# The inversion of a chunked delta-rule scan in 32x32 pieces, and channel sums taken with 32 weight columns

## The chip, the cores and the metric

The kernel runs on one core of one Trainium2 chip. The metric is the device time of one execution in microseconds; lower is better. The engines are TensorE (PE, with its weight loads listed apart as PEld), VectorE (DVE), ScalarE (ACT), GpSimd (POOL) and the DMA queues.

## The reference

One encoder layer over 1024 + 256 tokens of 1024 channels, in fp32. Its parts: an RMS norm; one input projection; 2-D neighbourhood attention; an RWKV-7 scan in both directions; projections and gates that merge the two branches; a squared-ReLU MLP. Only the scan is touched. Cut to it:

```
def step(S, inp):                       # for each head, N = 64, two directions
    r_t, w_t, k_t, v_t, a_t, b_t = inp
    sa = einsum('zdhij,zdhj->zdhi', S, a_t)
    S = S * w_t[..., None, :] + sa[..., :, None] * b_t[..., None, :] + v_t[..., :, None] * k_t[..., None, :]
    y = einsum('zdhij,zdhj->zdhi', S, r_t)
    return S, y

kk = kk * rsqrt(sum(kk * kk, axis=-1) + 1e-12)          # norm of k over the 64 channels of a head
y  = (y - mean) * rsqrt(var + GN_EPS) * ln_w + ln_b     # mean and variance over the same 64 channels
```

## The kernel before

The scan is `scan_mixer`. A pair of heads fills the 128 partitions (64 channels each), so 8 heads are 4 pairs (`CT`); the 1280 tokens are taken in 5 blocks of 256 (`NB`), and a block in 4 chunks of 64 tokens (`GR`, index `g`). Two directions run side by side (index `u`). That makes 20 steps (`q`), each with 4 chunks, each with 2 heads x 2 directions = four independent 64x64 problems.

Inside a chunk the recurrence becomes a triangular 64x64 system. It is inverted by doubling: Y starts as the exact inverse of the 2x2 blocks on the diagonal (mask `first`, L955), X is its transpose (`turn`, L556). Each of the 5 levels then doubles the size of the inverted diagonal blocks, from 2 to 4, 8, 16, 32 and at last 64. A level is

- `level_q` (L568): q = A^T X, four 64x64 products per chunk;
- a mask on DVE (L1053), which keeps the part of q that joins two blocks, giving Q1;
- `level_xy`: new X (L577) and new Y (L580) from Q1, four products each; the last level needs Y alone;
- a copy from PSUM to SBUF on ACT (L890; the last level L894), which the next level's q reads.

The order on PE is written out by hand. The four chunks are staggered, so that PE works on others while DVE and ACT have one: within level l it is q(0), xy of the level before for chunk 2, q(1), xy of the level before for chunk 3, q(2), xy(0), q(3), xy(1). Behind the levels come, for each chunk, the state products (L592 to L639), and between them the next block's Gram products (L525, `gram_products`) and transposes to tokens (L538 to L544). Their inputs are prepared by POOL (L429 to L462, `prepare`), which starts when the chunk's masks of the step before are done. DVE, ACT and POOL each execute their list in order.

Every matmul here is fp32; the profile lists it as two LDWEIGHTS and two MATMUL records. "64*64" in a row is the part of the array that is used, rows times columns of it.

Work on whole pairs is placed between levels of certain blocks (`side`, `side_late`). Two such jobs are norms over the 64 channels of a head, once for k (tile sc_nrm) and once for y (sc_std), for each of the 4 pairs. `by_head` (L650) multiplies each of ten 128-token tiles, as weights, with two columns of ones; ACT takes the square root of the 128x20 result; DVE inverts it (`inverse`, L960); POOL spreads it to 128x1280 (L466); `back` (L656) turns it with ten products with the identity. Six of the eight norms lie in block i = 1 of the loop; the first (k of pair 0) is ahead of the loop and the last (y of pair 3) behind it. In the loop `inverse` stands on DVE in level 2 between the masks of chunks 2 and 3.

Of the kernel before, what the change touches and what calls it, by code (L numbers as in the profile page):

```python
# [9 lines left out]
P = 128  # L10
# [24 lines left out]
GRAM_BANK, TOK_BANK, STATE_BANK, LORA_BANK = 4, 5, 6, 7  # L35
LEVELS = 5
DECAY = -0.6065306597126334
# [14 lines left out]
CN_N = 384  # L52
# [4 lines left out]
CS_I = CS_L + LEVELS * 2 * C  # L57
# [249 lines left out]
def scan_mixer(nc, lora, params, cn_scan, ident, ones, mean, sT):  # L307

    with ExitStack() as ctx:
# [3 lines left out]
        def sem(n):  # L313
# [7 lines left out]
        joins = cs[:, CS_L:CS_L + LEVELS * 2 * C].rearrange("p (l t) -> p l t", l=LEVELS)  # L321
        eye, neg_eye = cs[:, CS_I:CS_I + C], cs[:, CS_I + C:CS_I + 2 * C]
        wl = sb("sc_lora", [P, CT, 5, P])
        k1a, half_bias = sb("sc_k1a", [P, CT]), sb("sc_hb", [P, CT, 4])
        rk_ones = sb("sc_rk", [P, CT, P])
        norms = [sb(f"sc_n{n}", [P, 2 * NT]) for n in range(2)]
# [12 lines left out]
        XY = [sb(f"sc_xy{g}", [P, 2, 2, C]) for g in range(GR)]  # L339
        AI, Q1, PT, UT = ([sb(f"sc_{n}{g}", [P, 2, C]) for g in range(GR)]  # L340
# [6 lines left out]
        x_out = [units(g, 2 * C, C) for g in range(GR)]  # L347
        y_out = [units(g, 4 * C, C) for g in range(GR)]
# [4 lines left out]
        cs_in, lora_in, scaled = sem("cs_in"), [sem(f"lora_in{c}") for c in range(CT)], sem("scaled")  # L353
# [10 lines left out]
        sqk_ready, ss_ps, nrm_ready, rn_ready, rnb_ready, rnb_ps, kk_ready = (  # L364
            sem("sqk"), sem("ss_ps"), sem("nrm"), sem("rn"), sem("rnb"), sem("rnb_ps"), sem("kk"))
        mean_ps, yc_ready, sqy_ready, var_ps, std_ready, rs_ready, rsb_ready, rsb_ps, yn_ready = (
            sem("mean_ps"), sem("yc"), sem("sqy"), sem("var_ps"), sem("std"), sem("rs"), sem("rsb"),
# [5 lines left out]
        heads = (slice(0, HD), slice(HD, P))  # L373
        col = lambda ct, n: params[:, PM_RK + ct * NPC + n:PM_RK + ct * NPC + n + 1]
# [31 lines left out]

        def tiles_of(p):

            return range(GROUPS[p][0] // P, (GROUPS[p][0] + GROUPS[p][1]) // P)
# [9 lines left out]
        def _(pool):  # L419
# [44 lines left out]
            def spread(ready, turn, norm, buf, done):  # L464
                pool.wait_ge(ready, turn + 1)
                nc.gpsimd.tensor_copy(buf[:, :].rearrange("p (n t) -> p n t", t=C),  # L466
                                      norm[:, :].unsqueeze(2).to_broadcast([P, 2 * NT, C])).then_inc(done, 1)

# [12 lines left out]
            spread(rn_ready, 0, norms[0], nrm, rnb_ready)  # L481
            prepare(0)
            for q in range(STEPS):
                ct, i = divmod(q, NB)
                if q + 1 < STEPS:
                    prepare(q + 1)
                if i == 0 and ct > 0:
                    bonus_in(ct - 1)
                if i == 1 and ct > 0:
                    spread(rs_ready, ct - 1, norms[1], std, rsb_ready)  # L490
                if i == 1 and ct + 1 < CT:
                    spread(rn_ready, ct + 1, norms[0], nrm, rnb_ready)
                if i == 3 and ct > 0:
                    plus_bonus(ct - 1)
            bonus_in(CT - 1)
            spread(rs_ready, CT - 1, norms[1], std, rsb_ready)
# [3 lines left out]
        def _(pe):  # L500
# [48 lines left out]
            def turn(q, g):  # L549
# [4 lines left out]
                for u in range(2):  # L554
                    for rows in heads:
                        last = nc.tensor.matmul(x_out[g][rows, u, :], XY[g][rows, 1, u, :], eye[rows, :],  # L556
                                                start=True, stop=True)
                last.then_inc(x1_ps, 1)

            def level_q(q, l, g):  # L560
# [5 lines left out]
                for u in range(2):  # L566
                    for rows in heads:
                        last = nc.tensor.matmul(q_out[g][rows, u, :], AI[g][rows, u, :], XY[g][rows, 0, u, :],  # L568
                                                start=True, stop=True)
                last.then_inc(q_ps, 1)  # L570

            def level_xy(q, l, g):
                pe.wait_ge(q_ready, (q * LEVELS + l) * GR + g + 1)
                for u in range(2):
                    if l < LEVELS - 1:
                        for rows in heads:
                            nc.tensor.matmul(x_out[g][rows, u, :], XY[g][rows, 1, u, :], Q1[g][rows, u, :],  # L577
                                             start=True, stop=True)
                    for rows in heads:
                        last = nc.tensor.matmul(y_out[g][rows, u, :], Q1[g][rows, u, :], XY[g][rows, 1, u, :],  # L580
                                                start=True, stop=True)
# [66 lines left out]
            def by_head(bank, sq, sums, done):  # L648
                for n in range(NT):
                    last = nc.tensor.matmul(ps[:, bank, 2 * n:2 * n + 2], sq[:, n * P:(n + 1) * P],  # L650
                                            sums[:, 0:P:HD], start=True, stop=True)
                last.then_inc(done, 1)

            def back(bank, spread, p, done):
                for m, n in enumerate(tiles_of(p)):
                    last = nc.tensor.matmul(ps[:, bank, m * P:(m + 1) * P], spread[:, n * P:(n + 1) * P], ident,  # L656
                                            start=True, stop=True)
                last.then_inc(done, 1)

            def side(ct, i, l):  # L660
# [10 lines left out]
                if i == 1 and ct > 0 and l == 0:  # L671
                    pe.wait_ge(sqy_ready, ct * NG)
                    by_head(GRAM_BANK, std, mean, var_ps)
                if i == 1 and ct + 1 < CT and l == 1:
                    pe.wait_ge(tok_ready, n)
                    pe.wait_ge(sqk_ready, (ct + 2) * NG)
                    by_head(TOK_BANK, nrm, ones, ss_ps)
# [7 lines left out]
                if i == 2 and ct > 0 and p is not None:  # L685
                    if p == 0:
                        pe.wait_ge(rsb_ready, ct)
                    else:
                        pe.wait_ge(yn_ready, c * NG + 1)
                    back(GRAM_BANK, std, p, rsb_ps)  # L690
                if i == 3 and ct + 1 < CT and p is not None:
                    if p == 0:
                        pe.wait_ge(rnb_ready, ct + 2)
                    else:
                        pe.wait_ge(kk_ready, (ct + 1) * NG + 1)
                    back(GRAM_BANK, nrm, p, rnb_ps)
# [5 lines left out]
            def side_late(ct, i):  # L702
# [9 lines left out]
                if i == 2 and ct > 0:  # L712
                    back(TOK_BANK, std, 1, rsb_ps)
                if i == 3 and ct + 1 < CT:
                    back(TOK_BANK, nrm, 1, rnb_ps)
# [17 lines left out]
            by_head(GRAM_BANK, nrm, ones, ss_ps)  # L733
            lora_products(0, 0, 3)
            lora_products(0, 1, 3)
            pe.wait_ge(rnb_ready, 1)
            for p in range(NG):
                back(p, nrm, p, rnb_ps)
            pe.wait_ge(cs_in, 16)
# [6 lines left out]
            pe.wait_ge(kk_ready, NG)  # L746
# [60 lines left out]
            by_head(STATE_BANK, std, mean, var_ps)  # L807
            pe.wait_ge(rsb_ready, CT)
            for p in range(NG):
                back(p, std, p, rsb_ps)  # L810
# [5 lines left out]
        def _(act):  # L816
# [29 lines left out]
            def k_norm(ct, bank):  # L846
                act.wait_ge(ss_ps, ct + 1)
                nc.scalar.activation(norms[0][:, :], ps[:, bank, 0:2 * NT], ACT.Sqrt,
                                     bias=params[:, PM_EPS + 2:PM_EPS + 3]).then_inc(nrm_ready, 1)

            def y_std(ct, bank):
                act.wait_ge(var_ps, ct + 1)
                nc.scalar.activation(norms[1][:, :], ps[:, bank, 0:2 * NT], ACT.Sqrt,
                                     bias=params[:, PM_EPS + 1:PM_EPS + 2]).then_inc(std_ready, 1)
# [25 lines left out]
            for q in range(STEPS):  # L880
                ct, i = divmod(q, NB)
                more, ahead = q + 1 < STEPS, q + 2 < STEPS
                for g in range(GR):
                    act.wait_ge(x1_ps, q * GR + g + 1)
                    nc.scalar.activation(XY[g][:, 0, :, :], x_out[g], ACT.Copy).then_inc(x1_ready, 1)
                for l in range(LEVELS):
                    for g in range(GR):
                        act.wait_ge(xy_ps, (q * LEVELS + l) * GR + g + 1)
                        if l < LEVELS - 1:
                            nc.scalar.activation(  # L890
                                XY[g][:, :, :, :].rearrange("p n u t -> p (n u t)"),
                                ps[:, g, 2 * C:6 * C], ACT.Copy).then_inc(xy_ready, 1)
                        else:
                            nc.scalar.activation(XY[g][:, 1, :, :], y_out[g], ACT.Copy  # L894
# [1154 lines left out]
```

## Time and profile before

| | us |
|---|---|
| median of 3 runs (lowest, highest) | 2915.7 (2912.87, 2916.56) |
| the profiled execution, its own time | 2910.93 |
| its span, first to last instruction | 2909.2 |
| of the span: the scan's loop of 20 steps, 950 to about 1645 | about 695 |

| engine | busy us | share of the span |
|---|---|---|
| PE | 2653.8 | 91% |
| PEld | 2209.6 | 76% |
| DVE | 1241.4 | 43% |
| ACT | 668.9 | 23% |
| POOL | 827.3 | 28% |

The table says that PE works almost all the time. It does not say what a row of PE is made of: how much of a matmul's time is its columns and how much is the wait for results of DVE and ACT has to be read from the stretch of the scan itself. Times in the rows are microseconds from the start of the span, "ns" apart.

### The profile page before, as it was taken

To read this page: it belongs to the slowest core of one execution; us is meant where nothing else is said; L and a number is where in the kernel's file an instruction comes from. 1 tells how busy PE (TensorE), PEld (TensorE's weight loads), DVE (VectorE), ACT (ScalarE), POOL (GpSimd) and SP (SyncE) were. 2 spreads that over 40 slices of the span, in tenths; PEclk is the share of its full clock that TensorE was granted. 3 is DMA by queue.
4 is the path that set the end of the run, shared out by engine and by line. 5 is a ranking of instruction groups with operands and counts; after the bars stand their busy time and mean duration, and the time that the engine had idled before them with its cause. 6 is when DMAs were issued, how large, how long until landed. Compare 5 with 4: busy or idle time off the path is not lost. (4 is left out here: it accounts for less than half of the span.)

```text
span 2909.2 us, 68114 instructions
## 1 busy us (share of the span) xinstructions
PE 2653.8 (91%) x29216; PEld 2209.6 (76%) x29216; DVE 1241.4 (43%) x2236; ACT 668.9 (23%) x1544; POOL 827.3 (28%) x644
## 2 busy tenths in 40 slices
PE   3987997997997999999999799596999999999997
PEld 2885456886886899998989655485888888888886
DVE  5003663551111444444444322565445544544545
ACT  3101551110001444444444211131011001101102
POOL 1222113332332233232333000543233233333324
PEclk9998998998998999999999999798999999999999
DMA  4111102101221000000000143432011111101113
GB/s 119 42 44 38 32 17 81 42 22 62 86 85 57 4 4 4 3 4 3 4 3 4 40 152 116 150 123 80 29 43 36 36 36 43 36 29 50 36 43 130
DMA packets 60191, 143.10 MB, mean 49 GB/s; under 512 B 12112, under 2 KB 31184, under 8 KB 59472
## 3 DMA queue, kind: packets, MB, share of 16 engines
q1 hardware_dynamic: 46176, 114.36, 12.0%
q10 hardware_dynamic: 10256, 12.49, 1.4%
q0 software_dynamic: 3552, 13.11, 1.1%
q8 instruction: 177, 2.90, 0.4%
q14 instruction: 30, 0.25, 0.0%
HBM read 108.48 MB, written 31.46 MB: 48 GB/s over the span
## 5 line engine op out<-in xcount | busy, mean ns | idle before, releaser
L1905 DVE TENSOR_TENSOR f<-f,ff_pd 128x512 f32<-128x512 f32 x320 | 214.2, 684 | 153.2 <-PE ff_pd L94 153.1
L1891 DVE TENSOR_TENSOR ff_sq<-ff_rl 128x512 f32<-128x512 f32 (+1 forms) x96 | 102.8, 1071 | 295.6 <-ACT ff_rl L1852 295.6
L1852 ACT ACTIVATE ff_rl<-ff_pu 128x512 f32<-128x512 f32 (+1 forms) x96 | 50.6, 527 | 759.0 <-PE ff_pu L94 759.0
L580 PE MATMUL sc_ps<-sc_xy,sc_q 64*64 64x64 f32 x3200 | 198.1, 221 | 0.0
L1053 DVE TENSOR_TENSOR sc_q<-sc_ps,sc_cs 128x128 f32<-128x128 f32 x400 | 113.6, 290 | 163.5 <-PE sc_ps L568 162.5
L577 PE MATMUL sc_ps<-sc_q,sc_xy 64*64 64x64 f32 x2560 | 170.6, 222 | 0.0
L568 PE MATMUL sc_ps<-sc_xy,sc_ai 64*64 64x64 f32 x3200 | 160.0, 223 | 1.4 <-ACT sc_xy L890 0.9
L890 ACT ACTIVATE sc_xy<-sc_ps 128x256 f32<-128x256 f32 x320 | 122.5, 383 | 160.3 <-PE sc_ps L580 159.7
L580 PEld LDWEIGHTS sc_ps<-sc_xy,sc_q 64*64 64x64 f32 x3200 | 156.1, 137 | 2.1 <-issue 1.0
L94 PE MATMUL ff_pu<-h2h,ff_wu0h 128*128 128x512 f32 (+1 forms) x384 | 136.8, 356 | 14.2 <-POOL ff_wu0l L1800 14.2
L429 POOL TENSOR_SCALAR sc_fac<-sc_icl,params,sc_k1a 128x512 f32<-128x512 f32 x20 | 15.3, 767 | 432.3 <-DVE sc_xy L955 414.5
L568 PEld LDWEIGHTS sc_ps<-sc_xy,sc_ai 64*64 64x64 f32 x3200 | 125.6, 137 | 15.3 <-ACT sc_xy L890 11.8
L94 PE MATMUL ff_pu<-h2l,ff_wu0h 128*128 128x512 f32 (+1 forms) x384 | 136.5, 356 | 0.0
L94 PE MATMUL ff_pu<-h2h,ff_wu0l 128*128 128x512 f32 (+1 forms) x384 | 136.5, 356 | 0.0
L94 PE MATMUL ff_pu<-h2l,ff_wu1h 128*128 128x512 f32 (+1 forms) x384 | 136.0, 354 | 0.0
L94 PE MATMUL ff_pu<-h2h,ff_wu1h 128*128 128x512 f32 (+1 forms) x384 | 135.9, 354 | 0.0
L94 PE MATMUL ff_pd<-ff_wd0h,ff_gh 128*128 128x512 f32 x320 | 126.6, 395 | 10.2 <-DVE f L1905 10.2
L94 PE MATMUL ff_pu<-h2h,ff_wu1l 128*128 128x512 f32 (+1 forms) x384 | 135.8, 354 | 0.0
L577 PEld LDWEIGHTS sc_ps<-sc_q,sc_xy 64*64 64x64 f32 x2560 | 132.3, 138 | 1.3
L1797 POOL TENSOR_TENSOR ff_wd0h<-ff_wr,params 128x1024 fp32r<-128x1024 f32 x16 | 30.3, 1895 | 356.4 <-PE ff_pd L94 356.4
L94 PE MATMUL ff_pd<-ff_wd1h,ff_gh 128*128 128x512 f32 x320 | 124.7, 390 | 0.0
L94 PE MATMUL ff_pd<-ff_wd0l,ff_gh 128*128 128x512 f32 x320 | 124.7, 390 | 0.0
(275 smaller groups left out, 7246.3 us busy)
## 6 DMA issues: line engine op xcount, KB each, us to landing
ff_wr<-in_w_up SPq DMA_DIRECT2D x32, 512.0 KB, 3.2
ff_wr<-in_w_down SPq DMA_DIRECT2D x32, 512.0 KB, 3.2
g_dram<-gp_g ACTq DMA_DIRECT2D x16, 640.0 KB, 2.9
mb_gate<-g_dram SPq DMA_DIRECT2D x8, 1280.0 KB, 8.9
gp_w<-in_w_in SPq DMA_DIRECT2D x16, 512.0 KB, 3.5
sp_w<-in_w_in SPq DMA_DIRECT2D x15, 512.0 KB, 3.5
n_x<-in_x SPq DMA_DIRECT2D x10, 512.0 KB, 3.6
m_dram<-mb_mo POOLq DMA_DIRECT2D x8, 640.0 KB, 8.9
```

The lines of the kernel that those rows point to most:

```text
L94: mm = nc.tensor.matmul(out, stationary[a], moving[b], start=first and n == 0, stop=last and n == len(pairs) - 1)
L429: nc.gpsimd.tensor_scalar(fac[:, :, :], icl[:, :, :], col(ct, K_A), k1a[:, ct:ct + 1], ALU.mult, ALU.add).then_inc(prep_own, 1)
L568: last = nc.tensor.matmul(q_out[g][rows, u, :], AI[g][rows, u, :], XY[g][rows, 0, u, :], start=True, stop=True)
L577: nc.tensor.matmul(x_out[g][rows, u, :], XY[g][rows, 1, u, :], Q1[g][rows, u, :], start=True, stop=True)
L580: last = nc.tensor.matmul(y_out[g][rows, u, :], Q1[g][rows, u, :], XY[g][rows, 1, u, :], start=True, stop=True)
L890: nc.scalar.activation(XY[g][:, :, :, :].rearrange("p n u t -> p (n u t)"), ps[:, g, 2 * C:6 * C], ACT.Copy).then_inc(xy_ready, 1)
L1053: nc.vector.tensor_tensor(Q1[g][:, :, :].rearrange("p u t -> p (u t)"), ps[:, g, 0:2 * C], joins[:, l, :], ALU.mult).then_inc(q_ready, 1)
L1797: nc.gpsimd.tensor_tensor(to[0], wr[m % 2][:, :], zero_like(wr[m % 2][:, :], zero), ALU.add).then_inc(high_done, 1)
L1852: nc.scalar.activation(rl[u % 2][:, 0:tn], pu[b][:, 0:tn], ACT.Relu).then_inc(relu, 1)
L1891: nc.vector.tensor_tensor(sq[u % 2][:, 0:tn], rl[u % 2][:, 0:tn], rl[u % 2][:, 0:tn], ALU.mult).then_inc(squared, 1)
L1905: nc.vector.tensor_tensor(at, at, pd[d % 4][:, :], ALU.add).then_inc(added, 1)
```

## The change

Up to the fourth level all that is computed lies in the 32x32 blocks on the diagonal. The change computes only those, in tiles of 32x32 of the array.

- A 64x64 product becomes two of 32x32. The four "strips" of 32 partitions (two per head) use the four tiles on the diagonal of the array. `turn`, `level_q` and `level_xy` of levels 0 to 3 have eight products where they had four. Results are packed: X and Y of a chunk are 128x64 each (`XYQ`), so the ACT copy reads 128x128 where it read 128x256, and the DVE mask works on 128x64 where it worked on 128x128.
- Level 3 writes its 32x32 results into places in a 64x64 area of PSUM whose other parts are zero. The area is zeroed once ahead of the loop (a DVE memset of 128x1024, and PE waits on it). Its copy is 128x256 as before. Level 4 is as before, in 64x64.
- `by_head` is three products: the tokens are the moving operand (512 columns each), the weights are 32 columns of which two are used, and the results go to partitions 0, 32 and 64. ACT's square root and DVE's reciprocal then work on 96x512 where they worked on 128x20.
- POOL's spread is gone. `back` multiplies two rows of each piece with two rows of ones and gives 128 partitions x 512 (or 256) columns at once, one product where there were four (or two).

```
+        strips = [(slice(s * Q, (s + 1) * Q), slice(s % 2 * Q, (s % 2 + 1) * Q)) for s in range(4)]
...
                 for u in range(2):
-                    for rows in heads:
-                        last = nc.tensor.matmul(q_out[g][rows, u, :], AI[g][rows, u, :], XY[g][rows, 0, u, :],
-                                                start=True, stop=True)
+                    if l < LAST_LEVEL:
+                        for rows, own in strips:
+                            last = nc.tensor.matmul(qq_out[g][rows, u, :], AI[g][rows, u, own],
+                                                    XYQ[g][rows, 0, u, :], start=True, stop=True)
...
+                    for n, (small, wide) in enumerate(((xq_out[g], x_out[g]), (yq_out[g], y_out[g]))):
+                        for rows, own in strips:
+                            y1 = XY[g][rows, 1, u, own] if l == 0 else XYQ[g][rows, 1, u, :]
+                            q1 = Q1[g][rows, u, 0:Q]
+                            out = wide[rows, u, own] if l == LAST_LEVEL - 1 else small[rows, u, :]
+                            last = nc.tensor.matmul(out, *((q1, y1) if n else (y1, q1)), start=True, stop=True)
...
-            def by_head(bank, sq, sums, done):
-                for n in range(NT):
-                    last = nc.tensor.matmul(ps[:, bank, 2 * n:2 * n + 2], sq[:, n * P:(n + 1) * P],
-                                            sums[:, 0:P:HD], start=True, stop=True)
...
+            def by_head(bank, sq, done):
+                for p in range(NG):
+                    last = nc.tensor.matmul(ps[32 * p:32 * p + 32, bank, :], by_heads, sq[:, full_piece(p)],
                                             start=True, stop=True)
                 last.then_inc(done, 1)
+
+            def back(bank, norm, p, done):
+                w = GROUPS[p][1]
+                nc.tensor.matmul(ps[:, bank, 0:w], by_row[place(p), :], norm[place(p), in_piece(p)], start=True, stop=True
+                                 ).then_inc(done, 1)
...
-                nc.vector.reciprocal(norm[:, :], norm[:, :]).then_inc(done, 1)
+                nc.vector.reciprocal(norm[placed, :], norm[placed, :]).then_inc(done, 1)
...
+            dve.wait_ge(kk_ready, NG)
+            nc.vector.memset(ps[:, 0:GR, 4 * C:8 * C], 0.0).then_inc(zeroed, 1)
```

How the rows stand on PE, at the boundary of levels 3 and 4 of one step. Before, from q(0) of level 4 to the last Y (sc_q is Q1, sc_ai is A, the digit is the chunk, x2 and x4 are products):

```order
L568 MATMUL sc_ps<-sc_xy0,sc_ai0 64x64 x4
L577 MATMUL sc_ps<-sc_q2,sc_xy2 64x64 x2
L580 MATMUL sc_ps<-sc_xy2,sc_q2 64x64 x2
L577 MATMUL sc_ps<-sc_q2,sc_xy2 64x64 x2
L580 MATMUL sc_ps<-sc_xy2,sc_q2 64x64 x2
L568 MATMUL sc_ps<-sc_xy1,sc_ai1 64x64 x4
L577 MATMUL sc_ps<-sc_q3,sc_xy3 64x64 x2
L580 MATMUL sc_ps<-sc_xy3,sc_q3 64x64 x2
L577 MATMUL sc_ps<-sc_q3,sc_xy3 64x64 x2
L580 MATMUL sc_ps<-sc_xy3,sc_q3 64x64 x2
L568 MATMUL sc_ps<-sc_xy2,sc_ai2 64x64 x4
L580 MATMUL sc_ps<-sc_xy0,sc_q0 64x64 x4
```

The same place of the changed kernel:

```order
L569 MATMUL sc_ps<-sc_xy0,sc_ai0 64x64 x4
L586 MATMUL sc_ps<-sc_q2,sc_xyq2 32x32 x4
L586 MATMUL sc_ps<-sc_xyq2,sc_q2 32x32 x4
L586 MATMUL sc_ps<-sc_q2,sc_xyq2 32x32 x4
L586 MATMUL sc_ps<-sc_xyq2,sc_q2 32x32 x4
L569 MATMUL sc_ps<-sc_xy1,sc_ai1 64x64 x4
L586 MATMUL sc_ps<-sc_q3,sc_xyq3 32x32 x4
L586 MATMUL sc_ps<-sc_xyq3,sc_q3 32x32 x4
L586 MATMUL sc_ps<-sc_q3,sc_xyq3 32x32 x4
L586 MATMUL sc_ps<-sc_xyq3,sc_q3 32x32 x4
L569 MATMUL sc_ps<-sc_xy2,sc_ai2 64x64 x4
L578 MATMUL sc_ps<-sc_xy0,sc_q0 64x64 x4
```

The order of the work is the same; the products of levels 0 to 3 are twice as many, and the used part of the array now changes five times here (into 64, 32, 64, 32, 64) and once more between the 64x64 products of the step before and `turn`.

## Rows read from the trace of the kernel before

**Rows 1.** Busy time by engine in stretches: length, PE, PEld, DVE, ACT, POOL, granted clock, DMA.

```profile
950.00:1630.00 680.00, 670.22 (x18364) 624.03 (x18366) 314.93 (x903) 305.52 (x849) 211.22 (x260) 0.99 0.02 4
1227.80:1242.00 14.20, 14.20 (x432) 13.76 (x430) 6.16 (x20) 6.20 (x18) 12.78 (x14) 1.00 0.02 3
1157.00:1160.30 3.30, 3.30 (x57) 3.18 (x53) 0.59 (x3) 1.15 (x3) 3.30 (x5) 0.50 0.01 2
```

**Rows 2.** Groups by line: operation, tiles, shapes, count, busy us, mean ns, idle before.

```profile
L568 PE MATMUL sc_ps<-sc_xy,sc_ai 64*64 64x64 f32 x3200 | 160.0, 223 | 1.4 <-ACT sc_xy L890 0.9 <-ACT sc_xy L885 0.2
...
L1053 DVE TENSOR_TENSOR sc_q<-sc_ps,sc_cs 128x128 f32<-128x128 f32 x400 | 113.6, 290 | 163.5 <-PE sc_ps L568 162.5
...
L890 ACT ACTIVATE sc_xy<-sc_ps 128x256 f32<-128x256 f32 x320 | 122.5, 383 | 160.3 <-PE sc_ps L580 159.7
```

**Rows 3.** Who waited for whom in the scan's loop: us in total, times, longest.

```profile
PEld sc_ps L568 <- ACT sc_xy L890: 11.6, 31, 1.1
```

**Rows 4.** Timeline of one level: start, duration, engine, line, count, idle before.

```profile
1233.89 0.40 PE L568 MATMUL sc_ps<-sc_xy,sc_ai 64*64 64x64 f32 x8
...
1234.33 0.29 DVE L1053 TENSOR_TENSOR sc_q<-sc_ps,sc_cs 128x128 f32<-128x128 f32 x1 [0.41 <-PE sc_ps L568]
...
1234.47 0.28 PE L580 MATMUL sc_ps<-sc_xy,sc_q 64*64 64x64 f32 x4
...
1234.59 0.40 PE L568 MATMUL sc_ps<-sc_xy,sc_ai 64*64 64x64 f32 x8
...
1234.80 0.38 ACT L890 ACTIVATE sc_xy<-sc_ps 128x256 f32<-128x256 f32 x1 [0.32 <-PE sc_ps L580]
```

**Rows 5.** Timeline, 512 columns in two 64*64 tiles and in the full array.

```profile
321.58 1.07 PE L1290 MATMUL at_s<-sT,at_qb 64*64 64x512 f32 x4
...
1616.69 1.13 PE L645 MATMUL sc_ps<-sT,sc_lora 128*128 128x512 f32 x2
```

**Rows 6.** Timeline, a change of the used part of the array and back.

```profile
1229.74 0.28 PE L580 MATMUL sc_ps<-sc_xy,sc_q 64*64 64x64 f32 x4
...
1229.95 1.16 PE L656 MATMUL sc_ps<-cn,sc_nrm 128*128 128x128 f32 x8
...
1231.04 0.45 PE L568 MATMUL sc_ps<-sc_xy,sc_ai 64*64 64x64 f32 x8
```

**Rows 7.** Timeline, first q of a step's levels and first product behind them.

```profile
1227.84 0.87 PE L568 MATMUL sc_ps<-sc_xy,sc_ai 64*64 64x64 f32 x24
...
1243.45 0.28 PE L592 MATMUL sc_ps<-sc_tk,sc_gm 64*64 64x64 f32 x4
```

**Rows 8.** Groups by line, of half the width of the mask's and of the copy's tiles.

```profile
L1369 DVE TENSOR_SCALAR sT<-at_o 128x64 f32<-128x64 f32 x80 | 17.6, 220 | 7.0 <-PE at_o L1313 6.6
...
L894 ACT ACTIVATE sc_xy<-sc_ps 128x128 f32<-128x128 f32 x80 | 21.3, 277 | 14.0 <-PE sc_ps L580 10.6
```

**Rows 9.** Timeline, a sum by head in the loop.

```profile
1153.20 2.39 PE L650 MATMUL sc_ps<-cn,sc_std 128*128 128x2 f32 x20
...
1155.52 0.45 PE L568 MATMUL sc_ps<-sc_xy,sc_ai 64*64 64x64 f32 x8
```

**Rows 10.** Timeline, one group of 24 products' records in the stretch behind that sum.

```profile
1157.05 0.65 PE L568 MATMUL sc_ps<-sc_xy,sc_ai 64*64 64x64 f32 x8
...
1158.33 0.65 PE L568 MATMUL sc_ps<-sc_xy,sc_ai 64*64 64x64 f32 x8
```

**Rows 11.** Groups by line: reciprocals of two widths.

```profile
L1358 DVE RECIPROCAL at_st<-at_st 128x1 f32<-128x1 f32 x80 | 12.7, 158 | 4.9 <-ACT at_pr L1329 4.7
...
L960 DVE RECIPROCAL sc_n<-sc_n 128x20 f32<-128x20 f32 x8 | 2.0, 271 | 17.2 <-ACT sc_n L853 8.8 <-ACT sc_n L848 8.5
```

**Rows 12.** Timeline, the first and the last norm, outside the loop.

```profile
913.77 4.42 PE L650 MATMUL sc_ps<-cn,sc_nrm 128*128 128x2 f32 x20 [5.91 <-ACT sc_nrm L839]
...
918.97 1.25 POOL L466 COPY sc_nrm<-sc_n 128x1280 f32<-128x1280 f32 x1 [34.23 <-DVE sc_n L960]
...
1653.30 4.63 PE L656 MATMUL sc_ps<-cn,sc_std 128*128 128x128 f32 x20 [1.99 <-POOL sc_std L466]
```

More of the change, by code:

```diff
@@ L325, in scan_mixer @@
         rk_ones = sb("sc_rk", [P, CT, P])
-        norms = [sb(f"sc_n{n}", [P, 2 * NT]) for n in range(2)]
+        norms = [sb(f"sc_n{n}", [P, 512]) for n in range(2)]
         AR = [sb(f"sc_ar{n}", [P, 4, 2, BT]) for n in range(2)]
@@ L339, in scan_mixer @@
         XY = [sb(f"sc_xy{g}", [P, 2, 2, C]) for g in range(GR)]
+        XYQ = [sb(f"sc_xyq{g}", [P, 2, 2, Q]) for g in range(GR)]
         AI, Q1, PT, UT = ([sb(f"sc_{n}{g}", [P, 2, C]) for g in range(GR)]
@@ L672, in side @@
                     pe.wait_ge(sqy_ready, ct * NG)
-                    by_head(GRAM_BANK, std, mean, var_ps)
+                    by_head(GRAM_BANK, std, var_ps)
                 if i == 1 and ct + 1 < CT and l == 1:
@@ L676, in side @@
                     pe.wait_ge(sqk_ready, (ct + 2) * NG)
-                    by_head(TOK_BANK, nrm, ones, ss_ps)
+                    by_head(TOK_BANK, nrm, ss_ps)
                 if i == 1 and ct > 0 and l == 2:
@@ L732, in _ @@
             pe.wait_ge(sqk_ready, NG)
-            by_head(GRAM_BANK, nrm, ones, ss_ps)
+            by_head(GRAM_BANK, nrm, ss_ps)
             lora_products(0, 0, 3)
             lora_products(0, 1, 3)
-            pe.wait_ge(rnb_ready, 1)
+            pe.wait_ge(rn_ready, 1)
+            pe.wait_ge(cs_in, 16)
             for p in range(NG):
-                back(p, nrm, p, rnb_ps)
-            pe.wait_ge(cs_in, 16)
+                back(p, norms[0], p, rnb_ps)
             pe.wait_ge(nrm_ready, 1)
@@ L806, in _ @@
             pe.wait_ge(sqy_ready, CT * NG)
-            by_head(STATE_BANK, std, mean, var_ps)
-            pe.wait_ge(rsb_ready, CT)
+            by_head(STATE_BANK, std, var_ps)
+            pe.wait_ge(rs_ready, CT)
             for p in range(NG):
-                back(p, std, p, rsb_ps)
+                back(p, norms[1], p, rsb_ps)
             pe.wait_ge(bv_ready, CT * NG)
@@ L1938, in encoder @@
         params, cn = sb("params", [P, PM_N]), sb("cn", [P, CN_N])
-        ident, ones, mean = (cn[:, c:c + P] for c in (CN_ID, CN_ONES, CN_MEAN))
+        ident, ones, mean, by_row = (cn[:, c:c + P] for c in (CN_ID, CN_ONES, CN_MEAN, CN_ROWS))
+        by_heads = cn[:, CN_HEADS:CN_HEADS + 32]
         with nc.semaphore("const_in") as const_in, nc.Block() as block:
@@ L1984, in host_constants @@
     for l in range(LEVELS):
-        parts += [joins(d, 4 << l).T + one for d in range(2)]
+        size = Q if l < LAST_LEVEL else C
+        parts += [np.tile((joins(d, 4 << l).T + one)[0:size, 0:size], (C // size, 1)) for d in range(2)]
     parts += [one, -one]
```

118 lines of the change are left out of this document (63 added, 55 removed).

## The prediction, made before the changed kernel ran

> **What bounds the kernel now.** I read the stretches first. In the scan's loop PE is busy 670.2 of 680 us at a granted clock of 0.99, while DVE and ACT are at 315 and 306 [rows 1]. Within the levels of one step PE is busy all of 14.2 us. So the question is what fills PE there. The groups by line [rows 2] give the shapes: each q group is 64x64, each mask 290 ns on DVE, each copy 383 ns on ACT, and both engines stand idle before them until PE delivers. The waits say the reverse for PE: it waited only 11.6 us in the whole loop for the copies, 31 times [rows 3]. The timeline [rows 4] gives the rate: the q group at 1233.89 and the next at 1234.59 are one turn of q and xy of one chunk apart, 8 + 16 = 24 MATMUL records in 0.70 us, or 29.2 ns for a record.
>
> What are 29.2 ns made of? Two records of 512 columns in the full array take 1.13 us, and four records of 512 columns in two 64*64 tiles take 1.07 us [rows 5]. A record costs two cycles of 2.4 GHz for a column (512 columns 427 ns, two records 854 ns and the end of the pipeline), and two tiles run side by side, else the four would take 1.7 us. So a 64-column record occupies its tile for 53.3 ns, the tile takes a new one every 58.3 ns, and two tiles give 29.2.
>
> **What the change does to the levels.** Levels 0 to 3 have, for a chunk, 16 + 32 records of 32 columns where they had 8 + 16 of 64. By the same reckoning a record occupies its tile for 26.7 ns and, with the same 5 ns on top, the tile takes one every 31.7 ns. If all four tiles on the diagonal run side by side, a record costs 7.9 ns: q 0.13 us, xy 0.25 us, a turn of both 0.38 us instead of 0.70.
>
> Then PE no longer hides the other engines. From the end of xy to the next q of the same chunk there lie: the pipeline and the start of the copy (the last four records before the copy start at 1234.47, the last of them about 0.06 later, the copy at 1234.80 [rows 4]: 0.27 us, less 0.03 for the narrower record), the copy of 128x128, 0.277 us [rows 8], then about 0.06 to PE and a weight load that is no longer hidden, 0.03. That makes 0.60 us. Between this xy and this q lie only one turn, less the q itself. With two chunks in flight at that point a turn lasts (0.38 + 0.60)/2 = 0.49 us: four turns, a level, 1.95 us, against 2.80 now. The other leg, q to mask to xy, is 0.2 + 0.22 [rows 8] + 0.09 = 0.51 us and fits into the two turns' worth that the order leaves it. DVE needs 4 x 0.22 and ACT 4 x 0.28 us a level; neither becomes the bound.
>
> Level 4 stays 64x64, 16 records a chunk (1.87 us of PE). But the used part of the array changes five times there. What a change costs is in rows 6: four records begin at 1229.74, the next group would follow 0.12 later and starts 0.21 later, so 0.09 us, and the weight load behind it is bare (0.03 for 32 columns, 0.05 for 64): 0.13 us, 0.7 in all; partly beside waits. Summed along the order: level 0 is entered with filled buffers, 1.46 us from its first q to that of level 1; three levels of 1.95; 0.1 for the wider copy of level 3: 7.4 us to the first q of level 4. From there four q groups of 0.23, two xy of level 3 (0.25), four y of 0.23, 0.65 for the changes and 0.1 of waiting, 3.1. In all 10.5 us.
>
> Before it is, from the first q at 1227.84 to L592 at 1243.45 [rows 7], 15.6 us, of which the two side jobs of that step take 1.9 (1.19 between 1229.86 and 1231.04 [rows 6], and a half as large one in level 2); 13.65 without. **Difference 3.1 us a step, 20 steps, 62 us.** `turn` is half as long, but its last chunk waits for the three masks that DVE makes behind the last Gram product, either way: nothing. POOL's `prepare` takes about 12.8 us from a step's start [rows 1]; the first Gram product that needs it comes behind the levels (10.5 us after the change) and all products of chunk 0 and the state's of chunk 1, some 3.5 us. It stays hidden, with 1 us to spare; should POOL be late, it costs what it is late. The memset of 128x1024 lies on DVE while POOL prepares the first block: nothing.
>
> **The norms,** eight of them, six in the loop. *Sum by head:* 20 records in 2.32 us (1153.20 to 1155.52 [rows 9]). After: six records of 512 columns in three column tiles; side by side 0.87 us, one after another 2.57. Two tiles that differ in rows and columns run side by side [rows 5]; I take the same of three that differ in columns alone, 0.95 with the change of mode: 1.4 x 6 = 8 us off. *Clock:* behind those sums the granted clock is 0.50 [rows 1], the lower level, 1.2 GHz, and the turn takes 1.28 us instead of 0.70 [rows 10]. What PE did before it fell was 20 records of two columns each. The loop's mean clock of 0.99 means that 680 x 0.01, at most x 0.015, us are lost this way; I take 8.5, five spans like that one. With 512 moving columns I count them as gone. *Back:* eight records take from 1229.95 to 1231.04 [rows 6], 0.136 us each, 20 of them 2.7 us; after, 1280 columns at 0.83 ns twice, 2.15 us: 3 us off in six.
>
> *Reciprocal:* this goes up. 128x1 takes 158 ns and 128x20 271 [rows 11]. By the slope, 5.9 ns for an element, 96x512 takes 3.2 us; bounds are 1.04 ns an element as in other DVE operations (0.7 us) and all of the 271 ns put on 20 elements (6.9 us). DVE is in order, chunk 3's mask stands behind it, and xy(3) and then everything on PE behind that: 2.9 us each, 6 in the loop, 17 us on. In pairs 1 and 2 two stand together, and PE is idle for 6 us; there the clock may fall after all: 5 us on. ACT's root of 512 instead of 20 columns: 0.3 x 6 = 2 on. The Trainium skill ("VectorE: DVE Perf Modes", section on the fixed hardware budget) says that the reciprocal is an iterative divide with a repeat count of 8. By that, at the page's 0.96 GHz, an estimate is 4.3 us for each, and the sum would be 9 us higher.
>
> *Outside the loop* [rows 12] the sum takes 4.42 us at the lower clock, POOL's spread 1.25 and back 4.63; all become shorter or vanish (to about 2, 0 and 2), against 3.2 more for the reciprocal: 3 off at each end, 6 us.
>
> **Sum:** -62 -8 -8.5 -3 +17 +5 +2 -6 = -64 us (the terms give -63.5). The profiled execution took 2910.9; the median of the three runs is 4.8 above it, and the same difference on the median gives 2852 us.
>
> **The rivals.**
> *Records cost 9 to 13 ns* (two tiles at a time in pairs, or an issue of some 6 ns for a record's load and product each). Nothing in the trace runs more than two tiles, so nothing excludes it. At 11.3 ns a turn is 0.565 us, a level 2.26 and the step 1.4 us longer: 2880 us. The point from which the levels gain nothing is 13 ns a record: 4 x 192 records x 13 ns are 10 us, with level 4 the 13.65 of now; then only the norms are left, and the result is within a few us of before.
> *PE issues no faster than now,* the case on the other side. The fastest lasting rate in the trace is a record every 29.2 ns [rows 4]. If that is a limit on issue and not the two tiles' work, a level has 192 records and takes 5.6 us instead of 2.8; with the mode changes 12 us a step, 3150 us. Against it speaks that 29.2 ns is what the columns ask for. The place is any q group of levels 0 to 3, the price 0.47 us instead of 0.13; it decides from 13 ns. The Trainium skill ("TensorE: Matmul & The Clock Gate", section "Wait — 56ns, not 53.3ns?") states such a floor: start-to-start never below about 25 ns, however few the columns. Taken as a floor across tiles, an estimate is 4.8 us a level and some 3090 us; taken as one for a tile, it lies under the 31.7 ns above and changes nothing. No row here tells which.
> *The clock falls in the levels.* It fell behind records with two columns; 32 columns with gaps are nearer to that than 64 without. At 1.2 GHz a record costs 13.3 ns, a turn 0.65, level 4 a third more, and some 1.7 us of the work behind the levels is lost before it recovers: 2.5 us a step worse than before, 2964 us.
> *The reciprocal at its upper bound,* 6.9 us: 30 us more, 2882, still faster.
>
> **The chances.** The forecast (levels bound by the copy's leg) 0.50; records at 9 to 13 ns 0.18; about even 0.04; issue above 13 ns 0.17; clock 0.07; reciprocal high, with the rest as forecast, 0.04. What a measurement can tell from no change is 0.2%, 6 us. Faster are the first, the second and the last, less a little: 0.70; same 0.05; slower 0.25. The forecast's own range is 2830 to 2880. To 2825 downwards lies a free reciprocal and a level nearer to 1.7 us. Upwards I go to 2945, which takes in the even case and small losses, and leaves out most of the two slow ones.
>
> **What would show it.** Right: q groups of 16 records starting about 0.13 us before the next group, PEld waiting on the ACT copy in every turn, PE's busy share in the loop falling to some 80%, levels of 1.95 us; `by_head` rows under 1 us, no stretch of clock 0.50 behind them; a reciprocal of about 3 us with PE idle behind it. Wrong: records evenly 13 ns or more apart with DVE and ACT still waiting for PE; a granted clock of 0.5 in the levels; `by_head` at 2.6 us; POOL's last product (L462) releasing the Gram products.

## The result: slower by 6.5%

The changed kernel took 3106.4 us (median of four runs, 3095.4 to 3109.5), the kernel before 2915.3 (2912.9 to 2916.6). The ratio is 1.065, with a 95% interval of 1.062 to 1.068. I had forecast 2852 us. Its profiled execution took 3105.6 us with a span of 3103.8.

The stretches of the changed kernel come first: length, busy time of PE, PEld, DVE, ACT and POOL, granted clock, DMA. The first row is the scan's loop, which answers to the first of [rows 1]; the second is what lies ahead of it, the third what lies behind it.

```profile
954.00:1826.00 872.00, 693.86 (x26466) 600.80 (x26468) 311.98 (x902) 280.29 (x849) 201.87 (x254) 0.78 0.02 4
0.00:954.00 954.00, 815.33 (x5380) 648.16 (x5380) 314.67 (x642) 182.88 (x378) 229.06 (x200) 0.92 0.17 55
1826.00:3103.80 1277.80, 1167.49 (x5474) 927.75 (x5469) 617.80 (x693) 182.60 (x319) 384.27 (x183) 0.96 0.20 69
```

Both cuts lie at the first turn and at the end of the last step's levels, as in [rows 1]: 872 us against 680. So of the 195 us between the two profiled executions 192 are lost in the loop. A step takes 44.5 us instead of 34.9, and the part of it from the turn to the last level 27.0 instead of 17.7. PE has 178 us of idle time in the loop, where it had 10, and the granted clock is 0.78 instead of 0.99. DVE and ACT did what was forecast: the groups by line (busy us, mean ns, idle before) show the mask at 223 ns, the copy at 278, and the reciprocal at 3.33 us.

```profile
L1064 DVE TENSOR_TENSOR sc_q<-sc_ps,sc_cs 128x64 f32<-128x64 f32 x320 | 68.6, 223 | 250.0 <-PE sc_ps L565 249.7
...
L894 ACT ACTIVATE sc_xyq<-sc_ps 128x128 f32<-128x128 f32 x240 | 66.7, 278 | 286.1 <-PE sc_ps L586 286.1
```

```profile
L968 DVE RECIPROCAL sc_n<-sc_n 96x512 f32<-96x512 f32 x8 | 26.5, 3334 | 15.0 <-ACT sc_n L857 8.4 <-ACT sc_n L852 6.6
```

Both engines still wait for PE. What does PE wait for? The longest of its waits (us in total, times, longest) name no engine:

```profile
PEld sc_ps L586 <- issue: 119.7, 75, 2.6
...
PEld sc_ps L565 <- issue: 74.5, 55, 2.6
```

"issue" is a wait for nothing that the profile shows. Before, the wait that led in PE's levels was the one for the copy, 11.6 us [rows 3]. The timeline of a level (start, duration, engine, line, count, idle before) shows what it looks like:

```profile
1404.70 0.33 PE L565 MATMUL sc_ps<-sc_xyq,sc_ai 32*32 32x32 f32 x16
1404.85 0.24 PE L586 MATMUL sc_ps<-sc_q,sc_xyq 32*32 32x32 f32 x8
...
1405.15 0.33 PE L565 MATMUL sc_ps<-sc_xyq,sc_ai 32*32 32x32 f32 x16
1405.30 0.23 PE L586 MATMUL sc_ps<-sc_q,sc_xyq 32*32 32x32 f32 x5
1407.49 0.26 PE L586 MATMUL sc_ps<-sc_q,sc_xyq 32*32 32x32 f32 x2 [1.96 <-issue]
...
1411.51 0.37 PE L565 MATMUL sc_ps<-sc_xyq,sc_ai 32*32 32x32 f32 x10 [2.06 <-issue]
```

The four tiles do run side by side: 16 records of a q group start in 0.15 us, and a whole turn of q and xy takes 0.45 (1404.70 to 1405.15). But in the row at 1405.30 PE stops in the middle of a group, after the fifth record of eight, where no semaphore is waited for. It goes on at 1407.49 and stops again.

What moves with these stops in the trace is queue q8, of kind "instruction". The page of the kernel before has the first of these rows, that of the changed one the second (packets, MB):

```profile
q8 instruction: 177, 2.90, 0.4%
```

```profile
q8 instruction: 240, 3.93, 0.5%
```

A packet is 16 KB, or 256 instructions of 64 bytes. In the trace's DMA records the packets of the changed kernel never start closer together than 3.3 us. Between the starts of two MATMUL records the loop has 118 gaps of more than 0.8 us, 206 us in sum (before: four, 6 us). The median stop begins 0.6 us after a packet has started and ends 1.4 us after one has landed. A 32-bit product is two weight loads and two MATMULs, so 256 instructions are 64 products, or 128 MATMUL records.

**Supply theory.** PE's instructions arrive in blocks of 256, each 3.3 to 3.8 us after the one before at the fastest. That is 13 to 15 ns an instruction and 27 to 29 ns for a record with its load, whatever the record does. The change doubles the instructions of levels 0 to 3, so they cannot be faster than that. **Rivals:** four small tiles side by side stall PE or pull the clock down by themselves (small-tile theory); the 3.3 us reciprocals do it (norms theory); a record has a fixed issue cost (issue-floor theory).

### The profile page after: what moved, and what is told of

Same layout as the page of the kernel before. It is cut to its first block and busy times, and to the rows that moved or that the text cites. A ratio compares the mean times of both kernels' runs of the same rounds, so it can differ in the third digit from the quotient of the medians.

```text
span 3103.8 us, 84300 instructions
## 1 busy us (share of the span) xinstructions
PE 2676.7 (86%) x37312; PEld 2176.7 (70%) x37312; DVE 1244.5 (40%) x2237; ACT 645.8 (21%) x1544; POOL 815.2 (26%) x636
## 5 line engine op out<-in xcount | busy, mean ns | idle before, releaser
L586 PE MATMUL sc_ps<-sc_q,sc_xyq 32*32 32x32 f32 x3840 | 136.5, 231 | 49.9 <-issue 40.8
L586 PE MATMUL sc_ps<-sc_xyq,sc_q 32*32 32x32 f32 x3840 | 136.2, 231 | 42.9 <-issue 42.8
L565 PE MATMUL sc_ps<-sc_xyq,sc_ai 32*32 32x32 f32 x5120 | 129.6, 221 | 47.1 <-issue 46.5
L1064 DVE TENSOR_TENSOR sc_q<-sc_ps,sc_cs 128x64 f32<-128x64 f32 x320 | 68.6, 223 | 250.0 <-PE sc_ps L565 249.7
L565 PEld LDWEIGHTS sc_ps<-sc_xyq,sc_ai 32*32 32x32 f32 x5120 | 97.5, 132 | 84.2 <-issue 74.5
L586 PEld LDWEIGHTS sc_ps<-sc_q,sc_xyq 32*32 32x32 f32 x3840 | 108.5, 143 | 55.0 <-issue 41.0
L586 PEld LDWEIGHTS sc_ps<-sc_xyq,sc_q 32*32 32x32 f32 x3840 | 110.4, 145 | 49.0 <-issue 49.0
L894 ACT ACTIVATE sc_xyq<-sc_ps 128x128 f32<-128x128 f32 x240 | 66.7, 278 | 286.1 <-PE sc_ps L586 286.1
L97 PE MATMUL ff_pd<-ff_wd0h,ff_gl 128*128 128x512 f32 x320 | 124.7, 390 | 0.0
```

Source lines behind the costliest of these rows:

```text
L97: mm = nc.tensor.matmul(out, stationary[a], moving[b], start=first and n == 0, stop=last and n == len(pairs) - 1)
L565: last = nc.tensor.matmul(qq_out[g][rows, u, :], AI[g][rows, u, own], XYQ[g][rows, 0, u, :], start=True, stop=True)
L586: last = nc.tensor.matmul(out, *((q1, y1) if n else (y1, q1)), start=True, stop=True)
L894: nc.scalar.activation(XYQ[g][:, :, :, :].rearrange("p n u t -> p (n u t)"), ps[:, g, 2 * C:4 * C], ACT.Copy).then_inc(xy_ready, 1)
L1064: nc.vector.tensor_tensor(Q1[g][:, :, 0:Q], qq_out[g], joins[:, l, :].rearrange("p (u t) -> p u t", u=2), ALU.mult).then_inc(q_ready, 1)
```

## The experiments

**Each part alone.** The two halves of the diff, without a line of new code. In the first the norms are those of before, in the second the levels.

```
 levels only:  x_out -> xq_out, strips, XYQ, joins_last, memset     norms as before
 norms only:   by_head, back, inverse on 96x512, no spread          levels as before
```

> Levels 0 to 3 and the turn in 32x32 tiles as in the changed kernel, the norms as before. Supply theory (PE stops because its instructions, fetched in blocks of 16 KB, come no faster than a block every 3.3 to 3.5 us, and the levels now ask for twice as many): the whole loss stays, 3105 us (3080 to 3130), granted clock about 0.89 to 0.90, and over 100 us of PE and PEld 'issue' waits on the level products. Norms theory (the 3.35 us reciprocal, with PE idle behind it, is what costs): the forecast's gain shows, 2850 us.

> The norms as in the changed kernel, all five levels in 64x64 tiles as before. Supply theory: by the terms of my sum (-8 -8.5 -3 +17 +5 +2 -6) about 2914 us (2900 to 2925), clock 0.96 to 0.97, no more issue waits than before. Norms theory: most of the 190 us, 3080 us or more.

Measured: levels alone 3110.7 us, ratio 1.068 (1.066 to 1.070); norms alone 2917.9 us, 1.0012 (1.0003 to 1.0021). The loss is in the levels. The norms theory falls, and the norms are within 4 us of the forecast for them.

**The streams.** No reference is computed here; PE runs 1024 products without any wait in them, written out or as 32 trips of a loop of 32 products.

```
 for r in range(256):                          # L1972, written out
     for rows, own in four: matmul(ps[rows, 4 + r % 2, 0:32], xs[rows, own], xs[rows, 64:96])
 with pe.Fori(0, 32) as i:                     # L1978, the same in a loop
     for r in range(8):
         for rows, own in four: matmul(...)
 # L1983, L1989: two tiles of 32x32; L1994, L2000: two of 64x64, 64 columns;
 # L2005, L2011: two of 64x64, 32 columns
```

> Only streams of small products on PE without any wait inside, nothing of the reference is computed (the input is copied to the output). Eight streams, each behind 24 products of 128x512: 1024 products (2048 records) of 32x32 tiles with 32 moving columns, four tiles in turn, written out, then the same in a hardware loop of 32 trips (128 instructions a trip); the same with two tiles of 32x32; with two of 64x64 and 64 columns; with two of 64x64 and 32 columns. Supply theory: written out, no stream is faster than 26 to 28 ns a record (2048 records 54 us), in the loop, whose body needs no new fetch, the four small tiles take about 8 ns a record, the two small ones 16, the 64x64 ones 29, written out or not. Issue-floor theory (a record costs PE 25 ns or more whatever it is): written out and in the loop are alike. For 64x64 with 32 columns I expect 27 to 29 ns in both, the weight load being the longer part.

The stretches of the eight streams, in the order of the program (length, PE, PEld, DVE, POOL, granted clock, DMA share and GB/s):

```profile
26.50:86.40 59.90, 29.55 (x2049) 27.61 (x2048) 0.00 (x0) 0.00 (x0) 0.54 0.02 4
111.60:139.90 28.30, 23.92 (x2049) 20.45 (x2048) 0.00 (x0) 0.00 (x0) 1.00 0.00 0
162.20:218.20 56.00, 53.61 (x2049) 52.36 (x2048) 0.00 (x0) 0.00 (x0) 0.55 0.02 4
242.30:277.60 35.30, 35.30 (x2049) 34.77 (x2048) 0.00 (x0) 0.00 (x0) 1.00 0.00 0
299.90:359.60 59.70, 59.70 (x2047) 59.70 (x2048) 0.00 (x0) 0.00 (x0) 1.00 0.02 4
381.90:441.70 59.80, 59.80 (x2049) 59.75 (x2048) 0.00 (x0) 0.00 (x0) 1.00 0.00 0
464.00:523.70 59.70, 59.70 (x2047) 59.69 (x2048) 0.00 (x0) 0.00 (x0) 1.00 0.02 4
546.00:605.70 59.70, 59.70 (x2047) 59.66 (x2046) 0.00 (x0) 0.00 (x0) 1.00 0.00 0
```

The same 2048 records in four small tiles take 59.9 us written out and 28.3 in the loop: 29.2 and 13.8 ns a record. Inside a trip a record takes 8.9 ns; the rest is 0.33 us from trip to trip. The timeline of the first stream has the same holes as the changed kernel, between bursts of exactly 128 records:

```profile
34.93 1.93 PE L1972 MATMUL st_ps<-xs 32*32 32x32 f32 x128 [2.29 <-issue]
38.94 1.93 PE L1972 MATMUL st_ps<-xs 32*32 32x32 f32 x128 [2.08 <-issue]
42.94 1.93 PE L1972 MATMUL st_ps<-xs 32*32 32x32 f32 x128 [2.08 <-issue]
46.40 1.92 PE L1972 MATMUL st_ps<-xs 32*32 32x32 f32 x128 [1.53 <-issue]
```

In that stretch the DMA view shows one queue, with 4096 instructions in 16 packets; in the loop's stretch it shows none at all.

```profile
DMA packets 16, 0.26 MB, mean 4 GB/s; under 512 B 0, under 2 KB 0, under 8 KB 0
...
q8 instruction: 16, 0.26, 1.8%
```

This shows the supply theory, and the issue floor falls: a record costs 8.9 ns when its instructions are there. The Trainium skill ("TensorE: Matmul & The Clock Gate", section "Wait — 56ns, not 53.3ns?") has a floor of about 25 ns between starts; across four tiles these rows contradict it. The Trainium skill ("Runtime: NRT & Kernel Launch", section "Instruction fetch mechanics") says that engines fetch in blocks of 256 instructions, which the packets confirm, that PE's buffer holds 2048, and that the fetch is hidden behind the issue. The trace disagrees with the last point, and shows nothing of so deep a buffer: the first hole comes after 175 records, some 350 instructions. The trace has 449 records of PE and PEld up to it, and the first packet on q8 starts at 28.47 us, after PE has stopped, though the 24 long products ahead of the stream had left it time.

The rows also speak on the clock. It fell to 0.50 in the two streams of small tiles that have holes, and stayed at 1.00 in the two without, with the same tiles. Small tiles alone do not lower it in these streams. The third stream (two small tiles, written out) says less on the supply than the first: at the lower clock two tiles need 26.7 ns a record by themselves, twice the 13.3 ns of the first stream's bursts, and it took 27.3.

**The same number of instructions in large tiles.** Levels 0 to 3 of the kernel before, each product in two halves:

```
+for cols in halves if l < LEVELS - 1 else whole:
     for rows in heads:
-        matmul(q_out[g][rows, u, :], AI[g][rows, u, :], XY[g][rows, 0, u, :])
+        matmul(q_out[g][rows, u, cols], AI[g][rows, u, :], XY[g][rows, 0, u, cols])
```

> The kernel before, with each level product of levels 0 to 3 cut into two of 32 moving columns: the tiles stay 64x64, two side by side, the arithmetic is the same, the number of instructions in the levels is that of the changed kernel. Supply theory: issue waits appear and the time is near that of the changed kernel, 3070 us (3030 to 3110), with q8 at about 235 packets. Small-tile theory (32x32 tiles, or four of them side by side, stall PE or pull the granted clock down by themselves): PE pays only the fixed few ns for a record, about 1.3 ns more for each of them, 2935 us (2920 to 2950), no issue waits.

Measured: 3215.2 us, 1.103 (1.097 to 1.108). Both theories missed, and the run does not tell them apart. Its groups show PE busy, with next to no issue wait:

```profile
L570 PE MATMUL sc_ps<-sc_xy,sc_ai 64*64 64x32 f32 x5120 | 220.5, 232 | 0.3 <-ACT sc_xy L889 0.2
```

The last two streams say why. 64x64 tiles with 32 columns take 29.2 ns a record, exactly as with 64 columns, written out or in a loop. Halving the moving columns saves nothing there; that the weight load, as wide as before, is the reason is likely but not shown apart. So each level took PE twice as long, and PE asked for instructions just slowly enough to be supplied. The median step took 27.7 us from the turn to the last level where it takes 16.8 before, some 220 us in 20 steps, of the 300 by which the loop is longer. The rest goes with a clock at 0.50 for 212 us of the loop (17 us before), in five stretches. Four of them begin at a two-column sum by head, and in all five PE is busy throughout; the third:

```profile
1257.50:1305.30 47.80, 47.80 (x733) 45.37 (x734) 5.84 (x20) 7.66 (x19) 7.19 (x10) 0.50 0.01 2
```

So holes are not the only thing that goes with the lower clock.

**As many instructions as before, in small tiles.** The changed kernel with two strips of four, which leaves out half of the inversion in these levels:

```
-strips = [(slice(s * Q, (s + 1) * Q), slice(s % 2 * Q, (s % 2 + 1) * Q)) for s in range(4)]
+strips = [(slice(s * Q, (s + 1) * Q), slice(s % 2 * Q, (s % 2 + 1) * Q)) for s in (0, 2)]
```

> The changed kernel with two of the four 32x32 tiles on the diagonal left out in levels 0 to 3 and the turn (so half of the inversion of these levels is not computed): 32x32 tiles, but only as many instructions as before. Supply theory: the issue waits are gone, PE waits on ACT's copy, the clock stays at 0.95 or more, and the time is what I forecast for the change, 2850 us (2830 to 2875). Small-tile theory: the clock falls to 0.50 in the levels as in the changed kernel, 2960 us or more.

Measured: 2922.2 us, 1.0032 (1.0022 to 1.0041), 184 us faster than the changed kernel, with two small tiles instead of four. Since it halves the work of the array too, it is the streams and not this run that exclude the small-tile theory. And it is not the 2850 that I expected. In the loop:

```profile
950.00:1642.00 692.00, 657.73 (x18114) 577.59 (x18110) 308.70 (x899) 277.60 (x842) 200.59 (x252) 0.81 0.01 4
```

The long holes are gone (18 us of issue waits in the levels, PEld), yet the clock is 0.81. Where it is 0.50 a turn takes 0.64 us. To see whether the clock takes the gain, I gave the two idle tiles work into unused PSUM:

```
+if u == 0:
+    for rows, own in idle_strips:
+        matmul(ps[rows, LORA_BANK, 256:256 + 160], eye[rows, own], cs[rows, 0:160])
```

> The run with half the strips (half of the inversion of levels 0 to 3 left out), with two products of 160 moving columns into unused PSUM in the two idle 32x32 tiles of each q group: the tiles that lie idle work, with an eighth more instructions. If the low clock in the levels is what took the gain there: the clock stays higher and the time comes to 2860 us (2845 to 2890). If not, 2922 us or more, the clock still at 0.50 in the levels.

Measured: 2922.5 us, 1.0037. The clock rose as expected, the time stayed:

```profile
954.00:1642.00 688.00, 628.49 (x19476) 543.89 (x19470) 313.13 (x902) 278.79 (x849) 203.21 (x254) 0.92 0.02 4
```

At the full clock a level is now nearly as fast as forecast. The first records of q groups two chunks apart start 1.04 us after one another, 2.08 us for the level, where I had 1.95 and where it was 2.80 before the change:

```profile
1133.74 0.22 PE L566 MATMUL sc_ps<-sc_xyq,sc_ai 32*32 32x32 f32 x2
...
1134.78 0.22 PE L566 MATMUL sc_ps<-sc_xyq,sc_ai 32*32 32x32 f32 x2
...
1135.82 0.22 PE L566 MATMUL sc_ps<-sc_xyq,sc_ai 32*32 32x32 f32 x2
```

But issue waits came back with it:

```profile
PEld sc_ps L591 <- issue: 18.0, 22, 1.7
...
PEld sc_ps L566 <- issue: 8.8, 13, 1.6
```

A turn has 48 instructions and the filler's 8. In 0.52 us that is 9 ns an instruction (11 without the filler), faster than the 13 to 15 at which they arrive. The mean part from the turn to the last level is 17.6 us, as before. Clock and supply both stand in the way here; how the missing 70 us divide between them these two runs do not tell.

**Half the instructions for each product.** With bf16 operands a product is one load and one MATMUL. The first kernel does that in the 32x32 tiles of the change, the second in the 64x64 tiles of the kernel before (with the new norms in pieces, see below).

```
+XYQ, QQ, AB, Y0, eye_b = (bf16 tensors)            # 32x32: e6
+XB, QB, AB, Y0, eye_b = (bf16 tensors)             # 64x64: e10
+tensor_tensor(AB[g][:, :, :], GM[g][:, :, 0, :], eye.unsqueeze(1).to_broadcast([P, 2, C]), ALU.add)
```

> The changed kernel with bf16 operands in the turn and levels 0 to 3, so that a product is one load and one MATMUL instead of two of each (these levels are computed at bf16 precision; DVE makes one more 128x128 operation a chunk): four 32x32 tiles side by side, but half the instructions, as many in the levels as before. Supply theory: no issue waits; the levels are bound by the copy's leg, and as in the run with half the strips the granted clock falls to 0.50 in them, which matters less since a record is half as long: 2860 us (2840 to 2890). Small-tile theory (four tiles side by side stall PE): issue waits and 3000 us or more stay.

> The kernel before in its 64x64 tiles, with the new norms and the reciprocals in pieces, and with bf16 operands in the turn and levels 0 to 3 (these at bf16 precision, one more DVE operation a chunk): 12 records a chunk and level instead of 24, half the instructions of the kernel before there. Supply theory: instructions are no limit any more (0.32 us for a turn at 13.3 ns an instruction), the copy's leg is, 1.8 to 2.1 us a level instead of 2.80, the lower figure at the full clock: 2855 us (2830 to 2885), below the 32x32 version with twice the instructions. If small tiles are what makes levels fast, or if the clock falls so far that it takes the gain: 2890 us or more.

Measured: 2888.4 us for the small tiles, 0.992 (0.990 to 0.993), and 2829.8 us for the large ones, 0.972 (0.970 to 0.973), at the lower end of my range. The instructions of a chunk and level are 96 in the changed kernel, 48 before and in the first of these, 24 in the second. The time from the turn to the last level is 27.0, 17.7, 16.0 and 13.6 us, in this order. Part of my expectation for the small tiles was wrong: their issue waits did not vanish.

```profile
PEld sc_ps L591 <- issue: 26.5, 28, 1.8
...
PEld sc_ps L570 <- issue: 18.5, 20, 2.1
```

Since four small tiles with one pass each would let a level be shorter still, 48 instructions are again too many. In the large tiles, with 24, the wait for the copy leads:

```profile
PEld sc_ps L565 <- ACT sc_xb L888: 48.8, 106, 2.0
...
PEld sc_ps L565 <- issue: 6.9, 8, 1.7
```

That is the state which I had forecast for the change. The gain over the kernel before is not the instructions' alone: the new norms are in it, and bf16 makes a product shorter for the array as well. A turn of q and xy of one chunk takes 0.21 us of PE here, where it took 0.70 in fp32 [rows 4]:

```profile
1133.43 0.25 PE L565 MATMUL sc_ps<-sc_xb,sc_ab 64*64 64x64 bf16 x4
...
1133.64 0.23 PE L565 MATMUL sc_ps<-sc_xb,sc_ab 64*64 64x64 bf16 x4
```

The fair pair are these large tiles and the small ones with the same bf16 operands and the same norms in pieces (2877.1 us, the last run below): twice the instructions cost 47 us there.

**The norms.** They should have gained more. The timeline of the run with the norms alone shows where it went: two reciprocals in a row, and PE's next product behind them.

```profile
1165.19 6.56 DVE L949 RECIPROCAL sc_n<-sc_n 96x512 f32<-96x512 f32 x2 [2.58 <-ACT sc_n L842]
...
1171.95 0.48 PE L567 MATMUL sc_ps<-sc_q,sc_xy 64*64 64x64 f32 x4 [4.47 <-DVE sc_q L1042]
```

So I cut each into eight pieces, one behind a mask each. The second of the two moves to the next block as well, so they no longer stand in a row:

```
-if i == 1 and l == 2 and g == 2 and ct > 0: inverse(std_ready, c, norms[1], rs_ready)
-if i == 1 and l == 2 and g == 2 and ct + 1 < CT: inverse(nrm_ready, ct + 1, norms[0], rn_ready)
+if i == 1 and ct > 0 and 10 <= slot < 18: inverse_piece(std_ready, c, norms[1], rs_ready, slot - 10)
+if i == 2 and ct + 1 < CT and 4 <= slot < 12: inverse_piece(nrm_ready, ct + 1, norms[0], rn_ready, slot - 4)
```

> The norms as in the changed kernel, levels as before, and each reciprocal of the loop in eight pieces of 96x64, one behind a mask each, so that no mask waits 3.3 us. If PE's idle time behind the reciprocal and the clock that falls after it are what ate the gain of the norms: 2895 us (2888 to 2905), steps 2, 7, 12 and 17 back to those of before or shorter. If DVE's pieces delay the masks as much as the whole did: 2917 us.

Measured: 2900.0 us, 0.9960 (0.9947 to 0.9974), 18 us less than with whole reciprocals, though a piece costs DVE 0.54 us and all 48 of them 25.9 instead of 19.8. The mechanism holds; what the cutting gives and what the moving gives is not told apart. On top of the bf16 operands in small tiles:

> The run with bf16 operands in 32x32 tiles (levels 0 to 3 and the turn at bf16 precision), with each reciprocal of the loop in eight pieces. If the two gains add (the pieces took 18 us off the norms alone): 2870 us (2860 to 2880). If the pieces now delay the shorter turns of the levels: 2885 us or more.

Measured: 2877.1 us, 0.987 (0.986 to 0.989), inside the range of the first case, but by 11 of the 18 us.

## Why the prediction was wrong

**The step that failed** is the sentence on the rival "PE issues no faster than now": "Against it speaks that 29.2 ns is what the columns ask for". It was true of the array and said nothing of the instructions. 29.2 ns was the fastest lasting rate in the trace, and it was also, by coincidence, close to the rate at which instructions come. A level had 192 instructions (four chunks, 24 records each and their loads) in 2.80 us [rows 4], or 14.6 ns each; written out, the first stream gets one in the same 14.6. The levels were at both limits at once, and I saw one. The change halves what the array needs and doubles what must be fetched.

**The rival's price** was nearly right: 3150 us forecast for an issue at today's rate, 3106 measured. Its mechanism was not. I had thought of a cost for each record, which would space them evenly; the trace has bursts of 128 records, at 10 ns a record where the clock is full and 13.4 where it is at 0.50, and holes of 2 to 2.5 us. (The price of the rival at 11.3 ns was worked out from a turn of 0.565 us, where 48 records make 0.54; the conclusion does not hang on it.)

**The levels' terms.** A record's 7.9 ns is 8.9 in the loop of the second stream. Mask and copy came within 3 ns. The level of 1.95 us is 2.08 at its best with half the instructions. With all of them the median level is 5.4 us, from the first mask of one level to that of the next, close to the 5.6 of the rival; the same measure gives 2.85 before. The term of -62 us became +198, by the medians of the run with the levels alone and of the kernel before beside it.

**The clock.** I gave a fall in the levels 7%, as a cause of its own. It fell (0.78 in the loop), and where the holes stand it cost nothing. The changed kernel has seven bursts of 127 or 128 records between two stops at 10.2 ns a record and 31 at 13.4, which is the lower clock. From the start of a burst to the next start it is 3.80 us on the mean for the fast ones and 3.78 for the slow ones (3.64 and 3.63 in the run with the levels alone): a slower burst only has a shorter hole behind it. As to why it fell, the streams show it at 1.00 with the same tiles and no holes, so the supply is the likely cause here. But it is also at 0.50 for 47.8 us without a hole in the run with the columns split, and at 0.81 on the mean with half the strips, where the long holes are gone.

**The norms.** Forecast -1.5 us in all, measured +5.5 against 2912.4, the median of the kernel before beside it. The sum by head takes 0.99 us (0.95 forecast), the reciprocal 3.33 (3.2; the estimate of 4.3 is not borne out). The clock did worse than its term of -8.5 us: the loop of the run with the norms alone has 27 us at the lower clock, where it had 17. The stretches behind the sums are gone, but longer ones stand behind the reciprocals, for which I had put 5 us. Against the reciprocals' 17 + 5 us stand the 18 that the run in pieces gave back. How the missing 7 us divide among the terms is not shown.

**Outside the loop** the first sum by head begins at 913.8 us before [rows 12] and at 920.6 in the changed kernel, behind work that the change does not touch; in the runs with one part alone it begins at 917.3 and 917.4, so some us there are scatter. From that sum to the loop it is 36 us before and 32 after, and behind the loop 1279 and 1278. Of the -6 us some -5 are there.

## What to carry to other kernels

Count instructions as well as columns. For a long written-out stretch on TensorE, take its instructions (a 32-bit product is four) times 13 to 15 ns: if that is more than the array needs, expect smaller tiles to make it slower, however well they run side by side. A turn or two can run ahead of that rate (9 ns an instruction in the run with the filler), a whole scan did not. Of two kernels with the same bf16 arithmetic in the levels, the one with fewer, larger instructions won, 2830 us against 2877. A loop with a body of 128 instructions was not fetched again, at 0.33 us a trip. And where a long operation of a side job stands in an in-order queue, cutting it into pieces between the urgent ones can pay even when the pieces cost more in sum.

## What the runs showed of the hardware that I had not expected

- Instructions of PE come in packets of 16 KB, which start 3.3 us apart at the least in the changed kernel. Written out, a stream whose records need 29.2 ns each has no stop; one whose records need 8.9 ns stops after every 128 records, for 1.5 to 2.7 us.
- Four 32x32 tiles on the diagonal run side by side at 8.9 ns a record, at a granted clock of 1.00.
- In a 64x64 tile, 32 moving columns cost as much as 64: 29.2 ns a record with two tiles.
- A DVE reciprocal of 96x512 takes 3.33 us, 6.5 ns an element, and one of 96x64 0.54.
- The granted clock fell in streams with holes in them and not in the same streams without. With 64x64 tiles of 32 columns it also stood at 0.50 for 47.8 us in which PE was busy all the time.
- Where PE waits for its instructions the lower clock cost nothing: 3.78 us from one block of 128 records to the next at 13.4 ns a record, 3.80 at 10.2.
